# Narrow expert tiles read in whole rows through three 16 KB buffers, gate sums first, then up

## The chip, the cores and the metric

The kernel runs on one core of a Trainium2 chip. The metric is the device time of one execution in microseconds. Weights are read from HBM by the core's 16 DMA engines into SBUF (128 partitions), TensorE (PE) multiplies into eight PSUM banks, ScalarE (ACT) and VectorE (DVE) work on the results, GpSimd (POOL) does little here, and SyncE (SP) issues the weight transfers, in order, on one queue.

## The reference

Three blocks of transformer layers over 256 rows of width 1024. The change touches the mixture of experts of the second block alone: each row goes to two of eight experts, and each expert is a gated product with an inner width of 3584, in fp32.

```python
def swiglu(h, w_gate, w_up, w_down):
    return (jax.nn.silu(h @ w_gate) * (h @ w_up)) @ w_down

def moe_swiglu(h, w_router, we_gate, we_up, we_down):
    t = h.reshape(b * s, d)
    logits = (t @ w_router).astype(F32)
    top_val, top_idx = lax.top_k(logits, TOP_K)
    gates = jax.nn.softmax(top_val, axis=-1)
    combine = jnp.einsum('tk,tke->te', gates, jax.nn.one_hot(top_idx, N_EXPERTS, dtype=F32))
    for e in range(N_EXPERTS):
        y = y + combine[:, e:e + 1].astype(t.dtype) * swiglu(t, we_gate[e], we_up[e], we_down[e])
```

An expert's weights are 1024 x 3584 for gate and for up, 3584 x 1024 for down: 3 x 14 MB, 42 MB in all (1 MB is 1,048,576 bytes in this text).

## The kernel before

**Tiles.** The kernel sorts the rows by expert and works on tiles, each of one expert. A *wide* tile holds up to 128 rows and multiplies in three products of split operands: ACT makes a high part `WH` of each weight chunk (L1397), DVE the low part `WL` (L1401), PE takes WH with XTH, WL with XTH, WH with XTL (L567 to L569). A *narrow* tile holds up to 64 rows and multiplies the fp32 weights as they lie in the ring. The order is wide 0, narrow 0, wide 1, narrow 1, wide 2, narrow 2, narrow 3, narrow 4; each of the eight tiles reads its expert's 42 MB.

**Ring.** `ring` has six slots of 8 KB a partition (1 MB). A tile is read in 42 chunks of 1 MB. The order (`moe_order`) goes by pairs of column blocks: of pair 0 the gate chunks, then the up chunks; of pair 1 gate, up, then the down chunks of pair 0; and so on; pair 3 is half as wide. A gate or up chunk of pairs 0 to 2 is two blocks of 128 rows by 1024 columns, pieces of 4 KB; of pair 3 four blocks by 512 columns, pieces of 2 KB; a down chunk is two adjacent rows of 1024 a partition, 8 KB in one piece. SP issues a chunk when its slot is free: in a wide tile when DVE has made the low part of what lay there (`lo_made`), in a narrow one when PE has used it (`n_eaten`).

**Narrow tile.** For each pair p PE makes the gate sums into one bank (L3322), the up sums into another, and in between turns the columns of the pair before (L3333); ACT takes silu of the gate sums (L2175) and copies the turned columns (L2168), DVE multiplies with the up sums (L2686); PE makes the output sums of the pair before into bank 6 (L3345). In the gaps of this order stand the small steps of the other tiles: adding a wide or narrow tile's result to the rows (*scatter*, L1626 and L1622, with DVE's additions at L1634), and picking the rows of the next tiles (*selection*, L3303 for a wide tile, L3295 for a narrow one). Results of narrow tiles wait in four buffers `NY`, hidden columns in `NHID` and `NHT`.

**Wide tile 1** begins with the selection for narrow tile 1 (`first_of_1`), wide tile 2 without one.

Of the kernel before, what the change touches and what calls it, by code (L numbers as in the profile page):

```python
# [118 lines left out]
def build(nc, t):  # L119
    ctx = ExitStack()  # L120
    with ctx:
# [13 lines left out]
        QT = sb("QT", [128, 8, S])  # L135
        KT = sb("KT", [128, 8, S])
# [10 lines left out]
        neg_tri = sb("neg_tri", [128, 128])  # L147
        neg_ones = sb("neg_ones", [128, 128])
# [162 lines left out]

        landed = [sem(f"landed{s}") for s in range(RING)]
# [5 lines left out]

        def slot_ap(n, nk, width):
            return ring[:, n % RING, 0:nk * width].rearrange("p (k n) -> p k n", k=nk)  # L320
# [793 lines left out]
        n_landed = list(piece_in.values()) + [lam_in, rel_in]  # L1114
        assert len(n_landed) == RING
        n_landed_0 = [16] * len(piece_in) + [32, 64]
# [23 lines left out]
        IDX = pview(NEXP)  # L1140
        assert at_[0] <= 5120
# [19 lines left out]
        NSEL = P[:, 1, 2048:2176].rearrange("p (t s) -> p t s", t=2)  # L1161
        WSEL = P[:, 1, 2176:2432].rearrange("p (t s) -> p t s", t=2)
        XN32 = [P[:, 1, 1024 + 512 * b:1536 + 512 * b].rearrange("p (k r) -> p k r", k=KD) for b in range(2)]
        QT_FLAT, KT_FLAT = (x[:, :, :].rearrange("p k s -> p (k s)") for x in (QT, KT))
        NHID, NHT = ([QT_FLAT[:, at0 + 512 * b:at0 + 512 * b + 512] for b in range(2)] for at0 in (0, 1024))
        NY = [KT_FLAT[:, 512 * b:512 * b + 512] for b in range(4)]
        NCOMB = [P[:, 1, 2432 + S * b:2432 + S * b + S] for b in range(4)]
        MX = P[:, 1, 4096:5120]
# [450 lines left out]
        def scatter_narrow(out, j, half, tt):  # L1619

            side = slice(64 * half, 64 * half + 64)
            return nc.tensor.matmul(out[:, :], NCOMB[j % 4][side, tt * 128:tt * 128 + 128], NY[j % 4][side, :],  # L1622
                                    start=True, stop=True, skip_group_check=True)
# [21 lines left out]
        TURN_W, TURN_N = (1, 3), (1, 7)  # L1645
        SCATTERS = {0: ["wide"], 1: [0], 2: ["wide"], 3: [1], 4: [2, 3]}
# [10 lines left out]
        def eaten_by(j, key):  # L1657
            return j * MOE_CHUNKS + moe_at[key] + 1

        def pair_width(p):  # L1660
            return 256 * (pairs_[p][1] - pairs_[p][0])
# [20 lines left out]
        def _(sp):  # L1682
            def load(n):
# [3 lines left out]
                if N0 <= n < N0 + RING:  # L1687
                    sp.wait_ge(n_eaten, NARROW * MOE_CHUNKS - RING + n - N0 + 1)
# [55 lines left out]
            def load_wide(w, after_narrow):  # L1744

                e = expert_of(w)
                for c in range(MOE_CHUNKS):
                    n = N0 + c
                    if c < RING and after_narrow is not None:
                        sp.wait_ge(n_eaten, (after_narrow + 1) * MOE_CHUNKS + c - RING + 1)  # L1750
# [4 lines left out]

            def load_narrow(j, after_wide):

                e = expert_of(TILE_MAX + j)
                for c in range(MOE_CHUNKS):
                    n, before = N0 + c, j * MOE_CHUNKS + c - RING  # L1760
                    if c < RING and after_wide is not None:
                        sp.wait_ge(lo_made, after_wide * MOE_CHUNKS + (MOE_CHUNKS + n - RING + 1))
                    elif before >= 0:
                        sp.wait_ge(n_eaten, before + 1)
                    sp.dma_start(slot_ap(n, *expert_chunk(n)), expert_rows(e, c)).then_inc(n_landed[c % RING], 16)
# [184 lines left out]
        def _(act):  # L1950
# [209 lines left out]
            def narrow_tile(j, next_columns, next_splits):  # L2160

                def hidden_copy(p):
                    at_ = len(pairs_) * j + p
                    act.wait_ge(n_T, n_T_0 + at_ + 1)
                    if at_ >= 2:
                        act.wait_ge(n_eaten, eaten_by(*((j, ("down", pairs_[p - 2][1] - 1, 1)) if p >= 2 else
# [1430 lines left out]
```

## Time and profile before

| | us |
|---|---|
| median of 3 runs (lowest, highest) | 1922.06 (1919.86, 1922.43) |
| span of the profiled execution, first to last instruction | 1919.0 |
| PE busy in it | 1791.2 |
| DVE busy, ACT busy | 1019.2, 832.1 |
| granted clock of PE over the span | 0.993 |

The profiled execution's span is 3.06 us under the median of the runs. The eight expert tiles take the stretch from about 680 to 1566 us. The profile's times are from one execution. A busy PE in the profile is not PE at its peak, since matmuls overlap; waits are put down to what came last.

### The profile page before, as it was taken

What the parts mean: (1) busy time and instruction counts of PE and PEld (TensorE: products, weight loads), DVE (VectorE), ACT (ScalarE), POOL (GpSimd) and SP (SyncE); (2) the same over time, 40 slices, a digit from 0 to 9 for tenths busy, and PEclk for the clock granted to TensorE, in tenths of its full rate; (3) what the DMA queues carried; (4) which work ended last, traced back from release to release, by engine and by line L of the source; (5) the groups of instructions that cost most, each with busy time, mean ns of one, the idle gap of its engine ahead of it and who ended that gap; (6) DMA issues with size and microseconds to landing.
All of it is one profiled execution on the core that took longest, in us unless ns stands there. A gap on an engine that the chain in (4) does not pass through costs nothing.

```text
span 1919.0 us, 23227 instructions
## 1 busy us (share of the span) xinstructions
PE 1791.2 (93%) x9052; PEld 1268.1 (66%) x9052; DVE 1019.2 (53%) x1494; ACT 832.1 (43%) x1122; POOL 105.3 (5%) x111
## 2 busy tenths in 40 slices
PE   7999999999999999988998989998787879999998
PEld 5887888888888778535883458823232237888877
DVE  7666676554578698313881158810000124477686
ACT  4544577534356477203770047600000025556564
POOL 0000210000000270000000000000000000200002
PEclk9999999999999999999999999999999999999999
DMA  9863636555543299999999999999999986624500
GB/s 367 311 219 129 213 141 221 186 197 188 185 165 121 91 347 413 341 413 409 396 369 386 408 406 356 363 388 410 412 408 411 412 319 220 218 68 156 181 1 34
DMA packets 169570, 526.74 MB, mean 274 GB/s; under 512 B 12385, under 2 KB 23669, under 8 KB 155126
## 3 DMA queue, kind: packets, MB, share of 16 engines
q1 hardware_dynamic: 164224, 511.91, 70.7%
q10 hardware_dynamic: 3990, 9.15, 1.3%
q0 software_dynamic: 1248, 4.21, 0.7%
q8 instruction: 72, 1.18, 0.2%
q14 instruction: 36, 0.29, 0.0%
HBM read 515.26 MB, written 9.98 MB: 274 GB/s over the span
## 4 chain that ended last, share of the span: by engine, by line
PE 71%; DMA 19%; DVE 6%; ACT 2%; issue 1%; POOL 1%; SPq 0%; POOLq 0%; DVEq 0%; ACTq 0%
PE bank L567 17%; PE bank L569 17%; PE bank L568 17%; DMA ring<-in_od_we_up 7%; DMA ring<-in_od_we_down 6%; PE bank L3322 5%; DMA ring<-in_od_we_gate 5%; PE bank L3345 2%; PE bank L793 2%; PE bank L780 1%; DVE WL L1401 1%; PE bank L385 1%; DVE P L1384 1%; PE bank L813 1%; PE bank L811 1%
## 5 line engine op out<-in xcount | busy, mean ns | idle before, releaser
L1401 DVE TENSOR_TENSOR WL<-ring,WH 128x2048 fp32r<-128x2048 f32 (+1 forms) x260 | 584.5, 2264 | 230.4 <-ACT WH L1397 228.7
L1397 ACT ACTIVATE WH<-ring 128x2048 fp32r<-128x2048 f32 x261 | 491.6, 1895 | 243.5 <-PE bank L569 233.0
L567 PE MATMUL bank<-WH,XTH 128*128 128x512 f32 (+1 forms) x1288 | 509.2, 395 | 20.8 <-DVE WL L1401 15.1
L569 PE MATMUL bank<-WH,XTL 128*128 128x512 f32 (+1 forms) x1288 | 500.9, 389 | 0.0
L568 PE MATMUL bank<-WL,XTH 128*128 128x512 f32 (+1 forms) x1288 | 500.4, 388 | 0.0
L3322 PE MATMUL bank<-ring,P 128*64 128x512 f32 (+1 forms) x1280 | 265.5, 547 | 52.2 <-DMA ring<-in_od_we_up 28.0
L567 PEld LDWEIGHTS bank<-WH,XTH 128*128 128x128 f32 x1288 | 243.4, 189 | 79.3 <-DVE WL L1401 21.6
L569 PEld LDWEIGHTS bank<-WH,XTL 128*128 128x128 f32 x1288 | 243.3, 189 | 50.8
L568 PEld LDWEIGHTS bank<-WL,XTH 128*128 128x128 f32 x1288 | 243.8, 189 | 47.5 <-issue 0.5
L3322 PEld LDWEIGHTS bank<-ring,P 128*64 128x64 f32 x1280 | 84.5, 136 | 220.3 <-issue 100.2
L2686 DVE TENSOR_TENSOR QT<-bank,QT 128x512 f32<-128x512 f32 (+1 forms) x20 | 12.5, 625 | 353.1 <-PE bank L3322 353.1
L2175 ACT ACTIVATE QT<-bank 128x512 f32<-128x512 f32 (+1 forms) x20 | 10.9, 544 | 371.2 <-PE bank L3322 371.2
L3345 PE MATMUL bank<-ring,QT 128*64 128x512 f32 x560 | 132.4, 601 | 19.9 <-DMA ring<-in_od_we_down 19.5
L567 PE MATMUL bank<-WH,HTH 128*128 128x512 f32 (+1 forms) x288 | 109.7, 381 | 0.0
L569 PE MATMUL bank<-WH,HTL 128*128 128x512 f32 (+1 forms) x288 | 108.8, 378 | 0.0
L568 PE MATMUL bank<-WL,HTH 128*128 128x512 f32 (+1 forms) x288 | 108.7, 377 | 0.0
L3345 PEld LDWEIGHTS bank<-ring,QT 128*64 128x64 f32 x560 | 37.1, 136 | 105.7 <-issue 72.0
L840 ACT ACTIVATE scr<-scr,nmax 128x128 f32<-128x128 f32 x120 | 53.2, 444 | 39.4 <-DVE nmax L859 39.4
L661 ACT ACTIVATE P<-bank,stat 128x512 f32<-128x512 f32 x54 | 34.2, 684 | 68.1 <-PE bank L569 67.8
L567 PEld LDWEIGHTS bank<-WH,HTH 128*128 128x128 f32 x288 | 54.2, 188 | 10.8 <-DVE WL L1401 0.5
L569 PEld LDWEIGHTS bank<-WH,HTL 128*128 128x128 f32 x288 | 54.2, 188 | 10.2
L568 PEld LDWEIGHTS bank<-WL,HTH 128*128 128x128 f32 x288 | 54.2, 188 | 9.7
(504 smaller groups left out, 1585.0 us busy)
## 6 DMA issues: line engine op xcount, KB each, us to landing
ring<-in_od_we_gate SPq DMA_DIRECT2D x112, 1024.0 KB, 10.9
ring<-in_od_we_up SPq DMA_DIRECT2D x112, 1024.0 KB, 11.2
ring<-in_od_we_down SPq DMA_DIRECT2D x112, 1024.0 KB, 12.9
ring<-in_w_in SPq DMA_DIRECT2D x18, 1024.0 KB, 9.2
ring<-in_fox_w_in SPq DMA_DIRECT2D x16, 1024.0 KB, 6.4
ring<-in_nsa_w_in SPq DMA_DIRECT2D x14, 1024.0 KB, 4.9
ring<-in_w_ada SPq DMA_DIRECT2D x12, 1024.0 KB, 10.3
ring<-in_ev_w_in SPq DMA_DIRECT2D x12, 1024.0 KB, 5.1
```

What stands on the lines that cost most here:

```text
L385: last = nc.tensor.transpose(self.at(i)[:, j * S + tt * 128:j * S + tt * 128 + 128], src(tt), ident[:, :])
L567: nc.tensor.matmul(out, x[0], wt[0][:, k, :], start=start, stop=False, skip_group_check=check)
L568: nc.tensor.matmul(out, x[0], wt[1][:, k, :], start=False, stop=False, skip_group_check=check)
L569: return nc.tensor.matmul(out, x[1], wt[0][:, k, :], start=False, stop=stop, skip_group_check=check)
L661: last = nc.scalar.activation(dest(tt), self.out(c, tt)[:, 0:width], func, scale=stat[:, self.scale + tt:self.scale + tt + 1] if self.scal ...
L780: last = nc.tensor.matmul(self.score_bank(i)[:, a:a + n], q[:, a:a + 128], k[:, 128 - 128 * t0:256], start=not self.pe_mask, stop=True, sk ...
L793: last = nc.tensor.transpose(bank[6 + j % 2][:, c * 128:c * 128 + 128], self.E[j % 4][:, c * 128:c * 128 + 128], ident[:, :])
L840: last = nc.scalar.activation(e, e, ACT.Exp, bias=nmax[:, i % 4, t0:t0 + 1], scale=-1.0, accum_out=rs[:, g % 2, t0, uu:uu + 1])
L1397: nc.scalar.activation(wh, slot_ap(n, nk, width), ACT.Copy).then_inc(hi_made, 1)
L1401: nc.vector.tensor_tensor(wl, slot_ap(n, nk, width), wh.bitcast(F32), ALU.subtract).then_inc(lo_made, 1)
L3322: last = nc.tensor.matmul(out[64 * side:64 * side + 64, 0:width], XN32[j % 2][:, nk * i + k, :], wt[:, k, width * side:width * side + widt ...
L3345: last = nc.tensor.matmul(bank[6][64 * side:64 * side + 64, :], NHT[at_ % 2][:, at_h:at_h + 64], wt[:, k, 512 * side:512 * side + 512], st ...
```

## The change

Wide tiles stay as they are. In a narrow tile the six slots of the ring become three buffers of two slots, 16 KB a partition (`HOMES`; a fourth and a fifth name are set up but unused, since `home_of` is `c % 3`). Gate and up are read in chunks of 128 whole rows, 14 KB a partition, eight for gate and eight for up; down in chunks of four adjacent rows a partition, 16 KB, six of them, and two of two rows, 8 KB. That makes 24 chunks instead of 42. A buffer is filled when its last user has been eaten; the first narrow chunks after a wide tile wait until both slots of the buffer are free, the first wide chunks after a narrow tile until the last user of the buffer that holds their slot is eaten.

The sums of all four pairs are now made chunk by chunk: gate sums of all columns into banks 0 to 3, then up sums into banks 4 to 6 and the other half of bank 3; only then the four products, the turned columns and the output sums into bank 7. ACT takes the four silus after the last gate chunk. The scatters, the turning of the gates, and the selections stand between the up chunks. The selection for narrow tile 1 moves from the start of wide tile 1 into narrow tile 0. Some buffers move to other places in SBUF, `NY` has two instead of four, so tile 2 scatters two results and tile 4 one.

```diff
+        narrow_order = [(what, k) for what in ("gate", "up") for k in range(KD)]
+        narrow_order += [("down", p, side) for p in range(len(pairs_)) for side in range(2)]
+        home_of = [[c % 3 for c in range(NARROW_CHUNKS)] for i in range(NARROW)]
...
-        SCATTERS = {0: ["wide"], 1: [0], 2: ["wide"], 3: [1], 4: [2, 3]}
+        SCATTERS = {0: ["wide"], 1: [0], 2: ["wide", 1], 3: [2], 4: [3]}
...
+        HOMES = [two_slots(N0 + 2 * d) for d in range(3)] + [QK[:, :, :].rearrange("p k s -> p (k s)"), P[:, 1, 1024:5120]]
...
                     if c < RING and after_narrow is not None:
-                        sp.wait_ge(n_eaten, (after_narrow + 1) * MOE_CHUNKS + c - RING + 1)
+                        sp.wait_ge(n_eaten, eaten(*uses(c // 2, after_narrow)[-1]))
...
+            def narrow_rows(e, key):
+                if key[0] != "down":
+                    return (gate if key[0] == "gate" else up)[e, 128 * key[1]:128 * key[1] + 128, :].rearrange("e p n -> p (e n)")
+                n = 2 * pair_width(key[1])
+                k0 = 1024 * key[1] + n // 2 * key[2]
+                return down[e, k0:k0 + n // 2, :].rearrange("e (p k) n -> p (e k n)", p=128)
...
-                for c in range(MOE_CHUNKS):
-                    n, before = N0 + c, j * MOE_CHUNKS + c - RING
-                    if c < RING and after_wide is not None:
-                        sp.wait_ge(lo_made, after_wide * MOE_CHUNKS + (MOE_CHUNKS + n - RING + 1))
-                    elif before >= 0:
-                        sp.wait_ge(n_eaten, before + 1)
-                    sp.dma_start(slot_ap(n, *expert_chunk(n)), expert_rows(e, c)).then_inc(n_landed[c % RING], 16)
+                for c, key in enumerate(narrow_order):
+                    d = home_of[j][c]
+                    before = uses(d, j, c)
+                    if d < 3 and after_wide is not None and d not in home_of[j][:c]:
+                        sp.wait_ge(lo_made, after_wide * MOE_CHUNKS + (N0 + MOE_CHUNKS - RING + 2 * d + 2))
+                    elif before:
+                        sp.wait_ge(n_eaten, eaten(*before[-1]))
+                    ap = narrow_rows(e, key)
+                    sp.dma_start(HOMES[d][:, 0:ap.shape[1]], ap).then_inc(n_landed[d], 16)
...
+                act.wait_ge(n_eaten, eaten_by(j, ("gate", KD - 1)))
+                for p in (LAST, 0, 1, 2):
+                    nc.scalar.activation(NHID[p], hidden_bank("gate", p)[:, 0:pair_width(p)], ACT.Silu).then_inc(n_silu, 1)
+                next_columns()
                 for p in range(len(pairs_)):
...
+                    act.wait_ge(n_T, n_T_0 + len(pairs_) * j + p + 1)
+                    nc.scalar.activation(NHID[p], turned_bank(p)[:, 0:pair_width(p)], ACT.Copy).then_inc(n_hT, 1)
...
+                dve.wait_ge(n_eaten, eaten_by(j, ("up", KD - 1)))
+                dve.wait_ge(n_silu, n_silu_0 + len(pairs_) * (j + 1))
                 for p in range(len(pairs_)):
...
+                    nc.vector.tensor_tensor(NHID[p], hidden_bank("up", p)[:, 0:pair_width(p)], NHID[p], ALU.mult).then_inc(n_mul, 1)
...
+                for k in range(KD):
+                    hidden_sums("gate", k)
...
+                for k in range(KD):
+                    hidden_sums("up", k)
+                    if k == 0:
+                        pe.wait_ge(n_silu, n_silu_0 + len(pairs_) * (j + 1))
+                    if k < len(steps):
+                        scatter(k)
+                    if k == len(steps):
+                        pe.wait_ge(n_selg, n_selg_0 + j + 1)
                         for tt in range(TT):
...
+                    at_ = k - len(steps) - 1
+                    if at_ in (0, 2) and at_ // 2 < len(picks):
+                        if at_ == 0:
+                            pe.wait_ge(ns_added, steps_made(j + 1))
+                        picks[at_ // 2]()
+                turn_hidden_columns(0)
+                for p in range(len(pairs_)):
+                    if p < LAST:
+                        turn_hidden_columns(p + 1)
+                    for of in range(2):
+                        output_sums(p, of)
...
-            narrow_tile(0, 2, [lambda: select_wide(1)])
-            wide_tile(1, first_of_1, nothing)
+            narrow_tile(0, 2, [lambda: select_wide(1), lambda: narrow_after_wide(1, 1)])
+            wide_tile(1, lambda: after_narrow(0, 2), nothing)
```

How this moves PE's instructions is seen in narrow tile 0. First its middle, before: sums of one pair (`ring,P`: weights and the tile's rows), turned columns (`ident,QT`), output sums (`ring,QT`), with the scatters (L1626) and the selection for wide tile 1 (L3303) among them.

```order
L3322 MATMUL bank<-ring,P 64x512 x16
L1626 MATMUL bank<-P 128x512 x2
L3345 MATMUL bank<-ring,QT 64x512 x16
L1626 MATMUL bank<-P 128x512 x2
L3322 MATMUL bank<-ring,P 64x512 x16
L3333 MATMUL bank<-ident,QT 128x128 x4
L3322 MATMUL bank<-ring,P 64x512 x16
L3303 MATMUL bank<-P,O 128x128 x16
L3345 MATMUL bank<-ring,QT 64x512 x16
```

The same stretch after, from up chunk 1 on (L3349 are the sums of a chunk, six instructions of 512 and two of 256 columns; L1648 is the scatter, L3404 turns the gates, L3330 and L3322 are the selections for wide tile 1 and narrow tile 1).

```order
L1648 MATMUL bank<-P 128x512 x2
L3349 MATMUL bank<-ring,P 64x512 x6
L3349 MATMUL bank<-ring,P 64x256 x2
L3404 MATMUL bank<-ident,P 128x128 x2
L3349 MATMUL bank<-ring,P 64x512 x6
L3349 MATMUL bank<-ring,P 64x256 x2
L3330 MATMUL bank<-negs,O 128x128 x16
L3349 MATMUL bank<-ring,P 64x512 x6
L3349 MATMUL bank<-ring,P 64x256 x2
L3349 MATMUL bank<-ring,P 64x512 x6
L3349 MATMUL bank<-ring,P 64x256 x2
L3322 MATMUL bank<-scr,O 128x64 x16
```

Between two small steps there now stands one chunk of the up sums, and both selections lie in this tile.

Second, PE at the end of narrow tile 0 and the start of wide tile 1 (L567), before:

```order
L3322 MATMUL bank<-ring,P 64x256 x16
L3333 MATMUL bank<-ident,QT 128x128 x4
L3322 MATMUL bank<-ring,P 64x256 x16
L3345 MATMUL bank<-ring,QT 64x512 x8
L3333 MATMUL bank<-ident,QT 128x128 x2
L3345 MATMUL bank<-ring,QT 64x512 x16
L3295 MATMUL bank<-P,O 128x64 x16
L567 MATMUL bank<-WH,XTH 128x512
```

And after (L3361 turns the hidden columns, L3369 are the output sums, L584 begins wide tile 1):

```order
L3349 MATMUL bank<-ring,P 64x512 x6
L3349 MATMUL bank<-ring,P 64x256 x2
L3361 MATMUL bank<-ident,P 128x128 x8
L3369 MATMUL bank<-ring,P 64x512 x16
L3361 MATMUL bank<-ident,P 128x128 x4
L3369 MATMUL bank<-ring,P 64x512 x16
L3361 MATMUL bank<-ident,P 128x128 x2
L3369 MATMUL bank<-ring,P 64x512 x24
L584 MATMUL bank<-WH,XTH 128x512
```

All output sums now follow the last up chunk, and between them and wide tile 1 there is no selection any more.

## Rows read from the trace of the kernel before

**Rows 1.** The page: span, and the chain's shares by engine.

```profile
span 1919.0 us, 23227 instructions
...
PE 71%; DMA 19%; DVE 6%; ACT 2%; issue 1%; POOL 1%; SPq 0%; POOLq 0%; DVEq 0%; ACTq 0%
```

**Rows 2.** Windows: stretch, its length, each engine's busy us, PE's clock, DMA share, GB/s.

```profile
890.00:1014.50 124.50, 123.23 (x570) 101.39 (x570) 105.61 (x61) 87.70 (x57) 0.00 (x0) 1.00 1.00 386
...
1246.00:1353.00 107.00, 93.38 (x444) 33.19 (x446) 9.10 (x20) 5.73 (x10) 0.00 (x0) 1.00 1.00 398
1353.00:1460.00 107.00, 88.55 (x424) 30.30 (x422) 6.94 (x13) 5.04 (x9) 0.00 (x0) 1.00 1.02 411
```

**Rows 3.** Waits of PE and SP, 1246 to 1566: us in total, times, longest.

```profile
PE bank L3322 <- DMA ring<-in_od_we_up: 17.9, 32, 1.2
PE bank L3322 <- DMA ring<-in_od_we_gate: 17.8, 29, 1.5
...
SPq L1765 <- PE bank L3322: 172.7, 84, 5.3
```

**Rows 4.** PE's timeline: start, length, instruction, idle time before and its releaser.

```profile
1074.59 1.94 PE L3322 MATMUL bank<-ring,P 128*64 128x512 f32 x8 [0.62 <-DMA ring<-in_od_we_up]
1077.14 1.94 PE L3322 MATMUL bank<-ring,P 128*64 128x512 f32 x8 [0.62 <-DMA ring<-in_od_we_up]
...
1431.94 1.95 PE L3322 MATMUL bank<-ring,P 128*64 128x256 f32 x16 [0.67 <-DMA ring<-in_od_we_gate]
...
1437.35 1.95 PE L3322 MATMUL bank<-ring,P 128*64 128x256 f32 x16 [0.67 <-DMA ring<-in_od_we_up]
...
1442.32 1.94 PE L3345 MATMUL bank<-ring,QT 128*64 128x512 f32 x8 [0.46 <-DMA ring<-in_od_we_down]
...
1452.26 1.94 PE L3345 MATMUL bank<-ring,QT 128*64 128x512 f32 x8 [0.46 <-DMA ring<-in_od_we_down]
```

**Rows 5.** DMA packets of 1353 to 1460, counted by size.

```profile
DMA packets 10618, 43.95 MB, mean 411 GB/s; under 512 B 669, under 2 KB 669, under 8 KB 8821
```

**Rows 6.** DMA issues of 1247.5 to 1249 (queue empty): count, size, us to landing.

```profile
ring<-in_od_we_up SPq DMA_DIRECT2D x1, 1024.0 KB, 5.0
```

**Rows 7.** SP's timeline: the issue into the sixth slot before narrow tile 0.

```profile
786.16 0.37 SPq L1765 DMA_DIRECT2D ring<-in_od_we_up  x1
```

**Rows 8.** PE's timeline: first and last chunks of narrow tiles.

```profile
789.88 7.09 PE L3322 MATMUL bank<-ring,P 128*64 128x512 f32 x32
...
888.45 1.94 PE L3345 MATMUL bank<-ring,QT 128*64 128x512 f32 x8 [0.46 <-DMA ring<-in_od_we_down]
...
1014.44 7.09 PE L3322 MATMUL bank<-ring,P 128*64 128x512 f32 x32
...
1245.93 7.09 PE L3322 MATMUL bank<-ring,P 128*64 128x512 f32 x32
...
1344.60 1.94 PE L3345 MATMUL bank<-ring,QT 128*64 128x512 f32 x8 [0.47 <-DMA ring<-in_od_we_down]
...
1560.17 1.94 PE L3345 MATMUL bank<-ring,QT 128*64 128x512 f32 x8 [0.46 <-DMA ring<-in_od_we_down]
```

**Rows 9.** PE's timeline: a scatter of narrow tile 0, a selection of narrow tile 1.

```profile
824.03 1.98 PE L1626 MATMUL bank<-P 128*128 128x512 f32 x4
...
1079.01 3.84 PE L3303 MATMUL bank<-P,O 128*128 128x128 f32 x32
```

**Rows 10.** Lines of 1353 to 1460: count, busy us, mean ns, idle before.

```profile
L2686 DVE TENSOR_TENSOR QT<-bank,QT 128x512 f32<-128x512 f32 x3 | 2.1, 692 | 71.9 <-PE bank L3322 71.9
...
L2168 ACT ACTIVATE QT<-bank 128x512 f32<-128x512 f32 x3 | 1.8, 598 | 0.4 <-PE bank L3333 0.3
```

**Rows 11.** PE's timeline: last chunk of narrow tile 1, first matmul of wide tile 2.

```profile
1113.13 1.94 PE L3345 MATMUL bank<-ring,QT 128*64 128x512 f32 x8 [0.45 <-DMA ring<-in_od_we_down]
1120.43 0.80 PE L567 MATMUL bank<-WH,XTH 128*128 128x512 f32 x1 [5.36 <-DVE WL L1401]
```

**Rows 12.** Windows: the start of wide tile 2, columns as in rows 2.

```profile
1118.00:1124.80 6.80, 4.37 (x10) 3.47 (x11) 6.47 (x3) 3.87 (x3) 0.00 (x0) 0.50 1.03 410
```

## What the change will do to the time: the prediction

> **What bounds the kernel now.** I first read the page's span and chain [rows 1]: TensorE holds 71% of the chain that ends last, DMA 19%. Then busy time by stage, to see where that DMA part lies [rows 2]: in the wide tile from 890 to 1014.5 TensorE is busy 123.23 of 124.50 us, so TensorE sets its pace; in the narrow tiles it is busy 93.38 and 88.55 of 107, while the DMA share is 1.00 and 1.02. The waits of the last three narrow tiles [rows 3] agree: TensorE waits for weights (17.9 us for up, 17.8 for gate), and SyncE waits 172.7 us for TensorE to free a buffer: all buffers are handed out, the transfers are the limit. So a narrow tile gains what its 42 MB arrive earlier, and a wide tile gains only if its first weights arrive earlier. Before, first matmul to arrival of the last chunk takes 98.6 us in the narrow tiles that follow a wide one (888.45 − 789.88, 1113.13 − 1014.44, 1344.60 − 1245.93); narrow to narrow, last arrival to last arrival takes 107.7 and 107.9 (1344.60, 1452.26, 1560.17) [rows 4, 8, 11]. I call the tiles N0 to N4, the wide ones between them W1 and W2.
>
> **Longer rows.** How fast rows of each length arrive is seen where TensorE waits for each chunk, so that its starts are the arrivals [rows 4]. One MB takes 2.55 us in 4 KB pieces (1074.59 to 1077.14), 2.705 in 2 KB pieces (1431.94 to 1437.35, two chunks) and 2.485 in 8 KB rows (1442.32 to 1452.26, four). A chunk is spread over 16 engines: 16, 32 and 8 pieces each. From 8 to 32 pieces the time grows by 0.22 us: 9.2 ns a piece, and the middle value lies on that line. Without pieces a MB would take 2.485 − 8 × 0.0092 = 2.411. That descriptors of 8 KB really go as one packet is seen in the packets of a tile [rows 5]: 10618 less 8821 leaves 1797 of 8 KB or more, the 14 down chunks × 128.
> The change reads gate and up in 14 KB rows, 16 chunks of 1.75 MB with 8 pieces an engine: 1.75 × 2.411 + 0.074 = 4.293 us each. Six down chunks of 2 MB in 16 KB rows: 4.896. Two of 1 MB as before: 2.485. Together 68.7 + 29.4 + 5.0 = 103.0 us a tile, against 24 × 2.55 + 4 × 2.705 + 14 × 2.485 = 106.8. That is 3.8 a tile, 19 for five, if nothing is lost. No row shows a packet of 14 KB; from below, the 8 KB rate would bound a tile at 42 × 2.485 = 104.4, from above 4 KB's at 107.1. I take the line through three lengths.
> The Trainium skill (DMA: Bandwidth & Descriptors, Where 436 GB/s comes from) puts a ceiling of 435 GB/s on the 16 ports. At that rate a tile's 44.0 MB would take 101.2 us by estimate, 1.8 less than my line; the rows above stay below it.
>
> **Three buffers instead of six: the gaps.** A refill is late unless it is issued early enough: a chunk issued on an empty queue lands 5.0 us later [rows 6], of which 2.55 is its transfer, so 2.45 are start-up. TensorE takes 7.09/4 = 1.77 us a MB plus 0.17 to drain (1.94 for one MB alone) [rows 4, 8], so 3.27 for a gate chunk and 3.7 for a 2 MB down chunk. In the steady state two chunks are queued behind the one that is used (8.6 us), so it may lag by 8.6 − 3.27 − 2.45 = 2.8 us before the DMA runs dry. Five places:
> 1. *Entry from a wide tile.* A buffer needs two slots free; the last was freed at 786.16, 3.7 us ahead of N0 [rows 7], so three buffers land by 792.9 but the fourth chunk can be issued only when the first is used: 3.3 + 2.45 + 4.29 = 10.05 after the tile's start. The 20 that follow take 85.8, so the last lands 95.9 after the start, against 98.6: a gain of 2.7, not 3.8.
> 2. *Up sums.* The scatters and selections now all stand among the up chunks. In N0 and N1: two scatters of 2.0 us, a transpose of 0.45 and two selections of 3.8 [rows 9], 12 us against the 1.2 that each chunk gives back. The lag reaches 3.4 after the first selection and 4.7 after the second; over the allowed 2.8 (4.0 beside the longer down chunk) that is 0.6 + 0.7 = 1.3 us of DMA gap. N2 has four scatters and one selection: 1.5. N3 has two and one: 0.5. N4: none. That takes it that ACT and DVE keep up with the steps.
> 3. *From up to down.* DVE's product (0.69), four transposes, ACT's copy (0.6) [rows 10] and semaphores stop TensorE for some 2.5 us where before they lay beside other sums. The next chunk lands 1.6 us after the up sums anyway, three chunks are under way: nothing for the DMA.
> 4. *Exit.* Behind the last 2 MB chunk only two of 1 MB are queued, 4.97 us; it is used 3.75 after it lands, plus 0.15 for SyncE and 2.45: 1.4 us gap after each of the five tiles.
> 5. *Clock.* W1 began with a selection that filled the wait for its first split weights; this goes to N0. W2 has no such step now: TensorE idles 5.36 us there, the granted clock falls to 0.50 (1.2 GHz) [rows 11, 12], and ten matmuls take 4.37 us, not ten times 0.22 (32 alike in 7.09 [rows 8]): some 2.1 lost in a tile that TensorE bounds. W1 will idle about 6 us, so I expect the same there: +2.1.
>
> **The sum.** N0: −2.7 + 1.3 + 1.4 = 0. W1: +2.1. N1: 0, less 0.4 because ACT no longer is late for W2's first chunk: −0.4. N2: −2.7 + 1.5 = −1.2. N3: 1.4 + 103.0 + 0.5 against 107.7: −2.8. N4: 1.4 + 103.0 against 107.9: −3.5. After N4 the first weights of the next layer come 1.3 later, and two small chunks behind a large one leave TensorE 0.4 later: +1.7. Sum −4.1 us. The span of 1919.0 becomes 1914.9; the median of the runs lies 3.06 above the span, so 1922.06 becomes **1918.0**.
>
> **The rivals.**
> A, the forecast: long packets pay 19, gaps and the clock eat most. For it: three lengths on a line; against: gaps are small differences of long times. Start-up of 2.3 to 2.6 and a W1 without clock drop move it from −8 to −2: 1914 to 1920.
> B, *the DMA never runs dry*: the gaps 2 and 4 (4.6 + 7) and the clock (2.1) vanish as well: −4.1 − 13.7 = −18: 1904. It needs a start-up under 1 us behind a queue, and the rows have 2.45 only on an empty one.
> C, *the gain ends at 8 KB*: 104.4 a tile, +1.4 × 5: +2.9 on balance: 1925. For it: no row holds longer packets.
> D, *slower: the up phase starves the ring*. TensorE's queue is in order: if a scatter or selection waits for DVE's additions or ACT's copies, the up chunks behind it stay unread, the buffers stay full and the DMA stops. Every us beyond the lag of 2.8 is lost one for one. With 2.5 us at each of the six selections' waits: +15, 1933. It decides from 8 us in all, since 4.1 is gained before. For it: before, these steps stood between whole phases, now one chunk (3.1 us) lies between them. Against: DVE is busy only 9 of 107 us [rows 2].
> E, *it doesn't do what it says*: rows are cut into 4 KB packets again; the tile takes 107.1, +4.1 × 5: 1939. Against: 8 KB goes whole [rows 5].
>
> **How the numbers follow.** About 0.2% (3.8 us) is what can be told from no change here. A 0.50, of it 0.33 below 1918.2 and 0.17 within; B 0.12, faster; C 0.15, within 0.12 and slower 0.03; D 0.16, slower 0.13 and within 0.03; E 0.07, slower. Faster 0.45, same 0.32, slower 0.23. The range leaves out half of B, half of D and E, and takes in C: 1906 to 1928.
>
> **What would show it.** Packets of 14336 and 16384 B in the narrow tiles, and up chunks every 4.3 us; 4.35 speaks for C, 4.46 for E. N3 and N4 near 105 and 104.4 from last to last arrival. TensorE's first gate chunks of N0 without a wait for three chunks only. A DMA gap of about 1.4 at each tile's end, and one behind the selections; if TensorE waits there for DVE or ACT, it is D. A clock of 0.50 at W1's start. I am wrong if the chunks don't arrive faster than 8 KB ones, or if the gaps are under 0.5 or over 3 us a tile.

## The result and the profile after

The changed kernel takes **1939.72 us** (median of five runs, 1935.5 to 1948.09) against 1922.06 (1919.86 to 1932.04, five runs beside it): ratio **1.010, 95% interval 1.0068 to 1.0133**. It is slower, and the forecast of 1918.0 (1906 to 1928) missed: direction and range. In the page of the changed kernel, span and chain, which answer to [rows 1], TensorE's share grew and DMA's shrank, although the tiles are longer:

```profile
span 1944.6 us, 22907 instructions
...
PE 73%; DMA 16%; DVE 6%; ACT 3%; issue 1%; SPq 0%; POOLq 0%; POOL 0%; DVEq 0%; ACTq 0%
```

The profiled execution took 1946.36 us itself, one of the longer of the five, and its span is 25.6 us above the one of before, where the medians differ by 17.7. Between the stages' first and last matmuls the 25.6 lie so:

| stage | before | after | difference |
|---|---|---|---|
| N0 | 100.5 | 104.6 | +4.1 |
| W1 | 118.7 | 120.8 | +2.1 |
| N1 | 100.6 | 104.6 | +4.0 |
| N2 to N4 | 316.2 | 327.0 | +10.8 |
| W0, which the change doesn't touch | 123.7 | 125.5 | +1.8 |
| from a tile's last sum to W1, to W2 and to the next layer | 21.4 | 24.1 | +2.7 |

W2 is the same (125.1 and 125.0: its clock fell before too, [rows 12]). W0 lies between 123.7 and 125.6 in the profiled runs of the kernels below, whatever they change. The rest is in the narrow tiles and their borders. The windows over N0, N1 and N3 of the changed kernel (stretch, length, each engine's busy us, PE's clock, DMA share, GB/s) answer to [rows 2]:

```profile
792.60:897.30 104.70, 91.32 (x457) 37.21 (x456) 10.71 (x26) 7.00 (x18) 0.00 (x0) 0.98 0.95 388
...
1023.70:1128.40 104.70, 90.00 (x457) 36.58 (x456) 10.71 (x26) 6.99 (x17) 0.00 (x0) 0.98 0.95 384
...
1365.00:1477.50 112.50, 90.59 (x426) 34.58 (x424) 6.75 (x13) 4.71 (x9) 0.00 (x0) 0.94 0.97 392
```

Before, the DMA share in the narrow tiles was 1.00 to 1.02, the clock 1.00, the rate 397 to 411 GB/s. Now the DMA runs dry: 0.95 to 0.97, and 384 to 392 GB/s. TensorE isn't the bound either, busy 90 of 104.7 us. TensorE's and SyncE's waits over N2 to N4 (us in total, times, longest) answer to [rows 3]:

```profile
PE bank L3349 <- DMA ring<-in_od_we_gate: 30.8, 15, 4.3
PE bank L3349 <- DMA ring<-in_od_we_up: 15.0, 11, 3.6
PE bank L3369 <- DMA ring<-in_od_we_down: 12.1, 13, 2.7
...
SPq L1810 <- PE bank L3349: 209.6, 48, 8.9
```

Both wait: TensorE for weights (30.8 us in the gate sums, before 17.8), and SyncE for TensorE to hand back a buffer (209.6, before 172.7). Both waited before too, but with the DMA always busy; now they wait while it runs dry. That points to a ring that is too short. How a gap looks is seen in TensorE's timeline, here N3's first gate chunks and its last up chunk (start, length, instruction, idle time before and its releaser):

```profile
1370.82 7.93 PE L3349 MATMUL bank<-ring,scr 128*64 128x512 f32 x32 [4.30 <-DMA ring<-in_od_we_gate]
1379.29 3.23 PE L3349 MATMUL bank<-ring,scr 128*64 128x512 f32 x16 [0.54 <-DMA ring<-in_od_we_gate]
1385.78 12.10 PE L3349 MATMUL bank<-ring,scr 128*64 128x512 f32 x48 [3.27 <-DMA ring<-in_od_we_gate]
1399.74 3.23 PE L3349 MATMUL bank<-ring,scr 128*64 128x512 f32 x16 [1.86 <-DMA ring<-in_od_we_gate]
...
1441.98 4.92 PE L3349 MATMUL bank<-ring,scr 128*64 128x512 f32 x16 [3.58 <-DMA ring<-in_od_we_up]
```

The chunk at 1385.78 comes 6.49 us after the one before it, not 4.29. TensorE had idled 4.30 us ahead of 1370.82; with the clock at 0.50 right after it, two chunks took 7.93 us, where two take 6.2 at full clock. The first buffer came back late, and three chunks on, where its next chunk is awaited, TensorE idles 3.27 us, and three further on 1.86.

I call a *gap* what a chunk lands later than the chunk before it plus its own transfer (4.29, 4.89 or 2.47 us). In the changed kernel's five narrow tiles the gaps over 0.3 us, from the fourth chunk of N0 to N2 on and over all of N3 and N4, add up to some 38 us: 5.5 at the fourth chunk of N0 to N2, 10.5 in the gate sums behind it, 11.5 in the up sums, 5.6 in the down sums, 4.9 at the tiles' last and first chunks. The kernel with four buffers, below, has 3.2.

### The profile page after: what moved, and what is told of

The parts are those of the page before. It is cut to its first block, busy times and chain, and to the rows that moved or that the text cites. A ratio compares the mean times of both kernels' runs of the same rounds, so it can differ in the third digit from the quotient of the medians.

```text
span 1944.6 us, 22907 instructions
## 1 busy us (share of the span) xinstructions
PE 1794.0 (92%) x9052; PEld 1284.8 (66%) x9052; DVE 1019.9 (52%) x1494; ACT 830.2 (43%) x1122; POOL 101.7 (5%) x111
## 4 chain that ended last, share of the span: by engine, by line
PE 73%; DMA 16%; DVE 6%; ACT 3%; issue 1%; SPq 0%; POOLq 0%; POOL 0%; DVEq 0%; ACTq 0%
PE bank L584 17%; PE bank L586 17%; PE bank L585 17%; PE bank L3349 8%; DMA ring<-in_od_we_down 5%; DMA ring<-in_od_we_up 5%; DMA ring<-in_od_we_gate 5%; PE bank L3369 2%; DVE WL L1423 2%; PE bank L810 1%; PE bank L797 1%; ACT WH L1419 1%; PE bank L3322 1%; PE bank L402 1%; DVE P L1406 1%
## 5 line engine op out<-in xcount | busy, mean ns | idle before, releaser
L584 PE MATMUL bank<-WH,XTH 128*128 128x512 f32 (+1 forms) x1288 | 510.5, 396 | 28.0 <-DVE WL L1423 22.6
L584 PEld LDWEIGHTS bank<-WH,XTH 128*128 128x128 f32 x1288 | 244.5, 190 | 87.9 <-DVE WL L1423 23.9
L3349 PE MATMUL bank<-ring,P 128*64 128x512 f32 (+1 forms) x768 | 158.4, 561 | 35.5 <-DMA ring<-in_od_we_gate 27.1
L1656 DVE TENSOR_TENSOR X<-bank,X 128x512 f32<-128x512 f32 x28 | 18.0, 685 | 287.2 <-PE bank L1644 203.5
L3369 PE MATMUL bank<-ring,P 128*64 128x512 f32 x560 | 130.5, 610 | 22.0 <-DMA ring<-in_od_we_down 21.6
L3349 PEld LDWEIGHTS bank<-ring,P 128*64 128x64 f32 x768 | 54.2, 141 | 140.6 <-issue 99.1
L3349 PE MATMUL bank<-ring,scr 128*64 128x512 f32 (+1 forms) x512 | 107.5, 570 | 27.0 <-DMA ring<-in_od_we_gate 17.1
L2213 ACT ACTIVATE P<-bank 128x512 f32<-128x512 f32 (+1 forms) x20 | 10.9, 544 | 233.7 <-PE bank L3361 233.6
L584 PE MATMUL bank<-WH,HTH 128*128 128x512 f32 (+1 forms) x288 | 109.7, 381 | 0.0
L3369 PEld LDWEIGHTS bank<-ring,P 128*64 128x64 f32 x560 | 43.9, 139 | 98.1 <-issue 93.2
L3349 PEld LDWEIGHTS bank<-ring,scr 128*64 128x64 f32 x512 | 37.1, 143 | 97.5 <-issue 67.5
L2209 ACT ACTIVATE P<-bank 128x512 f32<-128x512 f32 (+1 forms) x20 | 9.3, 550 | 177.4 <-PE bank L3349 177.4
```

The costliest lines, as they stand in the source:

```text
L584: nc.tensor.matmul(out, x[0], wt[0][:, k, :], start=start, stop=False, skip_group_check=check)
L3349: last = nc.tensor.matmul(hidden_bank(what, p)[64 * side:64 * side + 64, 0:width], XN32[j % 2][:, k, :], wt[:, 1024 * p + width * side:102 ...
L3369: last = nc.tensor.matmul(bank[7][64 * side:64 * side + 64, :], NHID[p][:, r * 128 + 64 * of:r * 128 + 64 * of + 64], wt[:, D * r + 512 * ...
```

## The experiments

Theory after the result: **three buffers hold too little ahead; every late use of a chunk empties the DMA queue.** Rivals: the new order of the sums does it; the clock that falls in the gaps does it; the long rows themselves do it. A fourth, code that is read beside the weights, was not tried by itself.

**Five buffers.** The two further homes stand in the code already and are unused.

```diff
-        home_of = [[c % 3 for c in range(NARROW_CHUNKS)] for i in range(NARROW)]
+        home_of = [[c % 5 for c in range(NARROW_CHUNKS)] for i in range(NARROW)]
```

> The changed kernel with one line more: the narrow tiles' chunks go round five 16 KB buffers (the fourth and fifth name that the change sets up) instead of three. Theory 1, three buffers are too few, so that each late refill is felt: with four chunks behind the one in use a refill may come 8.6 us later, the gaps at the exits, behind the selections and at the entry from a wide tile vanish, the narrow tiles come to about 103 to 105 us from last to last arrival, TensorE never idles 4 us in them and its clock stays at 1.0: about 1912 us, 25 to 30 under the changed kernel. Rival, the gaps come from TensorE's order (all gate sums, then up sums with the small steps among them) or from code loads whatever the depth: at most 10 us under the changed kernel, about 1930.

Measured 1905.36 us (1903.31 to 1909.24), ratio 0.9923 (0.9907 to 0.994): faster than both kernels, 34 us below three buffers, 7 below what I expected. N0, N1, N3 and N4 in its windows:

```profile
788.80:886.00 97.20, 89.11 (x457) 36.76 (x456) 10.72 (x26) 7.00 (x17) 0.00 (x0) 1.00 1.01 426
1011.70:1109.30 97.60, 88.00 (x457) 36.02 (x456) 10.72 (x26) 7.00 (x17) 0.00 (x0) 1.00 1.01 425
1337.30:1441.70 104.40, 86.55 (x428) 33.51 (x424) 6.75 (x13) 4.72 (x9) 0.00 (x0) 0.98 1.00 422
1441.70:1545.80 104.10, 83.48 (x396) 29.41 (x392) 5.55 (x10) 4.71 (x9) 0.00 (x0) 0.98 1.00 422
```

The same rows, sums, scatters and selections in the same order, and the DMA share is 1.00 again, at 422 to 426 GB/s. So the order of the sums is not what holds the DMA up. The clock didn't stay at 1.00, as I had expected: it is 0.98 in N3 and N4.

**Six buffers of 8 KB, the changed order.** The three 16 KB buffers are cut into six; gate and up rows come as 8 KB and 6 KB, and each piece is awaited and handed back by itself.

```diff
-        narrow_order = [(what, k) for what in ("gate", "up") for k in range(KD)]
+        narrow_order = [(what, k, h) for what in ("gate", "up") for k in range(KD) for h in range(2)]
...
-        home_of = [[c % 3 for c in range(NARROW_CHUNKS)] for i in range(NARROW)]
+        home_of = [[c % 6 for c in range(NARROW_CHUNKS)] for i in range(NARROW)]
...
-        HOMES = [two_slots(N0 + 2 * d) for d in range(3)] + [QK[:, :, :].rearrange("p k s -> p (k s)"), P[:, 1, 1024:5120]]
+        HOMES = [ring[:, slot_at(N0 + d), :] for d in range(6)]
```

> The changed kernel's order of sums, but the ring is six slots of 8 KB as before: a gate or up chunk is cut into 2048 and 1536 columns (pieces of 8 and 6 KB), a down chunk into two rows a partition (8 KB). 46 chunks a tile. Theory 1, the size of the refill against the ring: five small chunks lie behind the one in use, a refill may be late by some 6 us instead of 2.8, so the gaps vanish but for the entry; a tile takes about 104.7 at these lengths: near 1920, 15 to 20 under the changed kernel. Rival, the order of sums makes the gaps: within 5 us of the changed kernel's time.

Measured 1918.43 us (1916.32 to 1919.64), ratio 0.999: 21 us below the changed kernel with the same 48 KB of buffers and the same order. The rival of the order falls a second time.

**Idle matmuls in TensorE's waits.** They keep the clock up where TensorE waits: 9 before N3 and N4, 11 before W1 and W2.

```diff
+            def busy(count):
+                for _ in range(count):
+                    nc.tensor.matmul(bank[2][:, :], ident[:, :], O[:, 0, 0:512], start=True, stop=True, skip_group_check=True)
...
+                if j >= 3:
+                    busy(9)
                 for k in range(KD):
                     hidden_sums("gate", k)
...
                 pe.wait_ge(ns_added, steps_made(j + 1))
+                busy(11)
```

> The changed kernel with idle matmuls on TensorE (128x512 into a bank that nobody reads): nine before the first gate chunk of narrow tiles 3 and 4 (about 4.0 us, the time that TensorE waits there), eleven before the first matmul of wide tiles 1 and 2 (4.8 us of a wait of 5.3 to 6.3). They compute nothing that is used. Theory 2, the clock: TensorE falls to half after these waits, eats the next chunks slower, and that makes the next gap; with fillers it stays at 1.0 there: wide tiles 1 and 2 gain 2.1 each, the second and third gaps of narrow 3 and 4 (2.2, 1.1, 1.8, 1.1 us) shrink by 4 to 5 in all: about 9 under the changed kernel, near 1931. Rival, the clock is no cause of the gaps, only the depth of the ring is: 4 under it at most (wide tiles alone), and the gaps in narrow 3 and 4 as they were.

Measured 1945.67 us (1942.09 to 1946.28), ratio 1.0126 (1.011 to 1.0143), not the 1931 that the clock as main cause would give. The kernel was mis-sized, as TensorE's timeline before W1 shows:

```profile
896.87 9.71 PE L3337 MATMUL bank<-O,ident 128*128 128x512 f32 x22
906.01 0.79 PE L584 MATMUL bank<-WH,XTH 128*128 128x512 f32 x1
```

The eleven run as 22 and take 9.1 us, where the wait was 5.3: counted from the tile before, W1 starts 3.8 us later and W2 2.7, which eats the 1.7 us that each of the two tiles is shorter (119.0 and 123.3 against 120.8 and 125.0). In N3 and N4 they fit, and N2 to N4 take 5.1 less, 321.9. So I shortened them:

**Shorter idle matmuls.** 5 before N3, N4, W1 and W2, and 4 ahead of the fourth chunk of N0 to N2 (these fall on one of the four gate sums, which loses its first three chunks there).

```diff
                 for k in range(KD):
+                    if j >= 3 and k == 0:
+                        busy(5)
+                    if j < 3 and k == 3:
+                        busy(4)
                     hidden_sums("gate", k)
...
                 pe.wait_ge(ns_added, steps_made(j + 1))
+                busy(5)
```

> The changed kernel with three buffers, and idle matmuls in TensorE's waits, sized shorter than the waits: 5 (4.2 us) before the first chunk of N3 and N4 and before W1 and W2, 4 (3.3 us) before the fourth chunk of N0 to N2. The idle matmuls' sums are overwritten. Theory that the clock's fall makes the later gaps: the falls to 0.50 in N0 to N4 and at W1 and W2 vanish, W1 and W2 take 1.7 us less each, N2 to N4 5 to 7 us less, N0 and N1 1: about 1929 to 1931. Rival, the clock only falls where the DMA has already run dry, and the gaps come from three buffers: 1936 to 1940.

Measured 1934.75 us (1932.72 to 1940.39), ratio 1.0087 (1.0062 to 1.0113): between the two expectations, and its interval overlaps that of the changed kernel. The trace says more. TensorE at N3's start:

```profile
1360.34 4.56 PE L3337 MATMUL bank<-O,ident 128*128 128x512 f32 x10
1365.46 3.23 PE L3353 MATMUL bank<-ring,scr 128*64 128x512 f32 x16 [0.57 <-DMA ring<-in_od_we_gate]
1369.76 3.23 PE L3353 MATMUL bank<-ring,scr 128*64 128x512 f32 x16 [1.06 <-DMA ring<-in_od_we_gate]
1374.06 3.23 PE L3353 MATMUL bank<-ring,scr 128*64 128x512 f32 x16 [1.07 <-DMA ring<-in_od_we_gate]
```

Chunks come every 4.3 us, and the waits of 3.27 and 1.86 that the changed kernel had at the fourth and seventh are gone: the chain of clock, late hand-back and next gap is broken here. N2 to N4 take 319.8 us, 7.2 less. With four buffers they take 305.6. So the clock's fall multiplies the gaps and doesn't make them. Its price in the narrow tiles, 5 to 7 of the 34 us, rests on one profiled execution of each kernel; the medians differ by 5.0, W1 and W2 included.

**Selection back at W1's start**, where it stood before, out of N0's up sums.

```diff
...
-            narrow_tile(0, 2, [lambda: select_wide(1), lambda: narrow_after_wide(1, 1)])
-            wide_tile(1, lambda: after_narrow(0, 2), nothing)
+            narrow_tile(0, 2, [lambda: select_wide(1)])
+            wide_tile(1, first_of_1, nothing)
```

> The changed kernel with the selection for narrow tile 1 back at the start of wide tile 1, as before the change. Theory of the prediction's steps 2 and 5: the selection fills TensorE's wait, the clock stays at 1.0 at the start of wide tile 1 (2.1 us), and narrow tile 0 loses the gap behind its second selection (1.4): 3 to 4 under the changed kernel, about 1936. Rival, the place of the selection does not matter: within 1 us of it.

Measured 1940.91 us (1934.61 to 1943.18), ratio 1.0096: no difference. W1 starts 6.1 us after N0's end instead of 5.3, and its clock falls to 0.50 at 899.9 all the same.

**Four buffers.** As with five, with `c % 4`.

> Four 16 KB buffers in place of three, all else as in the changed kernel. Theory: the loss is lag. With three buffers a chunk may be used 2.8 us late before the DMA runs dry; a fourth adds one chunk, 4.29 us, so 7.1. The largest gaps in the changed kernel's five narrow tiles are 2 to 4.5 us, so nearly all go, and the time is within 2 us of five buffers: 1905 to 1908. Rival, each buffer brings a like share (from 1939.7 with three to 1905.4 with five): about 1922. Rival, the order of the sums holds the DMA up: above 1930.

Measured 1905.28 us (1903.85 to 1910.5), ratio 0.9925 (0.9908 to 0.9943): the same as five. Three buffers lose 34 us and the fourth gives it all back, so it is a threshold, not a share for each buffer. The fourth buffer isn't a slot of the ring, so its chunk doesn't wait for the wide tile either; TensorE at N0's start uses it, in `QK`, without a wait:

```profile
791.66 9.24 PE L3349 MATMUL bank<-ring,P 128*64 128x512 f32 x48
800.73 3.18 PE L3349 MATMUL bank<-QK,P 128*64 128x512 f32 x16
803.93 3.23 PE L3349 MATMUL bank<-ring,P 128*64 128x512 f32 x16
808.23 3.23 PE L3349 MATMUL bank<-ring,P 128*64 128x512 f32 x16 [1.06 <-DMA ring<-in_od_we_gate]
```

**A late use, added.** 5 idle matmuls into a free bank ahead of the second up chunk of each narrow tile, with three buffers and with four.

```diff
                 for k in range(KD):
+                    if k == 1:
+                        late(5)
                     hidden_sums("up", k)
```

> The changed kernel with three buffers, and in each narrow tile 5 idle matmuls (4.2 us, into a bank that is free there) ahead of the second up chunk: each later chunk of the tile is used that much later. Theory that the loss is lag: three buffers have none to spare, TensorE gives back 1.2 us a chunk only while the DMA is behind it, so the most of 4.2 us is lost in each of five tiles: 1939.7 + 12 to 21 = 1952 to 1961. Rival, the lag of 2.8 us that the prediction allowed is there in the up sums and takes the first 2.8 of the 4.2: 1939.7 + 5 by 1.4 = 1947 or less. Rival, the loss is elsewhere: 1940.

> The same 5 idle matmuls (4.2 us) in each narrow tile, with four buffers. The fourth adds 4.29 us to the lag that is allowed: theory, little of it is lost, 1905.3 + 0 to 5 = 1905 to 1910. Rival, TensorE's own time decides by now: 1905.3 + 21 = 1926.

With three buffers 1955.76 us (1953.65 to 1962.06), ratio 1.0194 (1.0174 to 1.0213): 16 us more, 3.2 of the 4.2 added in each tile. The allowance of 2.8 us is not there. N4 shows it best, where the up sums had no gap over 0.3 us: with the late use they have two, of 3.0 and 1.2, the whole of the 4.2. With four buffers they have none. With four 1916.24 us (1911.52 to 1926.77): 11 more than without, where I expected 0 to 5. So the fourth buffer covers what the kernel needs and, by these runs, about half of 4.2 us beyond; the threshold is close.

**Five buffers, shorter rows.** The same bytes into the same buffers by two DMAs a chunk, 8 KB and 6 KB, or 8 and 8.

```diff
...
-                    ap = narrow_rows(e, key)
-                    sp.dma_start(HOMES[d][:, 0:ap.shape[1]], ap).then_inc(n_landed[d], 16)
+                    at_ = 0
+                    for ap in parts_of(e, key):
+                        sp.dma_start(HOMES[d][:, at_:at_ + ap.shape[1]], ap).then_inc(n_landed[d], 16)
+                        at_ += ap.shape[1]
```

> Five 16 KB buffers, each chunk read by two DMAs: gate and up rows of 14 KB as 8 KB and 6 KB, the four adjacent down rows of 16 KB as 8 KB twice. Buffers, order and bytes as with five buffers and whole rows (1905.4). Theory of the prediction, 9.2 ns for each piece: 16 chunks by 8 pieces an engine and 6 chunks by 8 more, 176 by 9.2 ns = 1.6 us a tile, 8 us for five tiles: 1913. Rival, rows over 8 KB bring nothing: 1905 to 1907. Packets of 14336 and 16384 bytes are then gone.

Measured 1913.16 us (1911.35 to 1914.81), ratio 0.9966 (0.9953 to 0.9979): 7.8 us above five buffers with whole rows, forecast 8.0 (6.0 above their second measurement, below). Rows over 8 KB are worth about what the line through three lengths says, while the DMA never waits.

**Three buffers, shorter rows.** The same edit on the changed kernel: the buffers are still awaited and handed back whole.

> Three 16 KB buffers, each filled by two DMAs of 8 KB and 6 KB (or 8 and 8) a row, handed back only when the whole buffer is read. Against six 8 KB buffers (1918.4) the memory, the DMAs and the order of the sums are the same, and only the unit in which a buffer is awaited and handed back is doubled; against the changed kernel (1939.7) only the rows are shorter. Theory that the unit of three large buffers costs the loss, whatever the rows: 1939.7 + 8 (the pieces, as with five buffers) = 1945 to 1950. Rival, long rows themselves make a transfer land late behind a queue (longer start-up, engines that finish apart): near six buffers, 1918 to 1930.

Measured 1940.37 us (1936.61 to 1941.37), ratio 1.0089. Neither expectation. Against six small buffers, which have the same bytes, DMAs and order, it is 22 us slower: that is the price of the unit in which a buffer is awaited and handed back. N0 in the windows of both, first these three buffers, then the six small ones:

```profile
790.60:895.60 105.00, 90.15 (x457) 37.03 (x456) 10.72 (x26) 6.99 (x18) 0.00 (x0) 1.00 0.95 383
...
791.80:891.70 99.90, 90.91 (x457) 35.50 (x456) 10.72 (x26) 7.00 (x17) 0.00 (x0) 1.00 0.98 403
```

Against the changed kernel it is the same, though its pieces cost 8 more; so with three buffers the long rows lose elsewhere what they gain. From the fourth chunk on N3 and N4 have 1.3 and 0.5 us of gaps in place of 7.3 and 2.8; why, these runs don't tell.

**Idle matmuls before W1 and W2, five buffers.** `busy(5)` where the eleven stood.

> Five buffers, and 5 idle matmuls (4.2 us) in TensorE's waits of some 5 us before W1 and W2. The idle matmuls' sums are overwritten. If the fall of the clock there costs what the prediction says (2.1 us in each): 1905.4 less 4 = 1901. Rival, the cost is hidden behind the weights' splitting on ACT and DVE: 1905.

> Five buffers with 5 idle matmuls ahead of W1 and W2 once more, beside five buffers without them on the same chip. If the clock's fall at these two starts costs some 2 us each: 4 us below five buffers alone. Rival, something that differs from run to run is larger (its runs lay at 1900.6, 1904.5 and 1909.5 to 1912.0): no difference between the two that the runs can tell.

> Five 16 KB buffers alone, beside the last one: 1905 again, and 15 us below before.

The first time 1909.52 us (1900.57 to 1911.96), ratio 0.9942; the second 1903.10 (1901.89 to 1911.41), 0.9923 (0.9907 to 0.9939), beside five buffers alone at 1907.17 (1904.36 to 1916.37), 0.9945 (0.9928 to 0.9963). In the profiles W1 takes 118.8 against 120.7 us and W2 123.1 against 125.8, so 4.6 us are there; but the runs of the same kernel spread over 11 us, and the intervals overlap. Not settled. The version that surely beats both kernels is the change with four or five buffers, 0.55 to 0.77% below before in three measurements.

## Why the prediction was wrong

- **What bounds the kernel: right.** The narrow tiles wait for their weights; with five buffers, where those come sooner, N0 takes 97.2 us instead of 100.5 while W1 gains nothing (120.4 instead of 118.7).
- **Longer rows: right, to a few per cent.** A narrow tile of the changed kernel in packets, which answers to [rows 5]:

```profile
DMA packets 3463, 44.14 MB, mean 392 GB/s; under 512 B 384, under 2 KB 384, under 8 KB 384
```

  3463 packets in place of 10618, none of them of 2 to 8 KB: rows go whole. Gate and up chunks come every 4.29 to 4.30 us where nothing disturbs them (1365.46, 1369.76, 1374.06 above; 4.293 forecast), 16 KB ones every 4.89 (4.896). In the kernel with five buffers N3 and N4 take 104.4 and 104.1 us from last to last arrival, with one gap in each (1.6 and 1.1); 103.0 was forecast without gaps. Five buffers with shorter rows price the pieces at 7.8 for 8.0. Rivals C and E are out. The Trainium skill (DMA: Bandwidth & Descriptors, Where 436 GB/s comes from) sets 435 GB/s as ceiling of the ports; the 422 to 426 of five buffers stay below it, as the forecast had it.
- **Three buffers instead of six: the step that failed.** Its arithmetic allowed a chunk to be used 2.8 us late: 8.6 in the queue, less 3.27 of use, less 2.45 of start-up. The start-up was read from a 1 MB chunk in 4 KB pieces on an empty queue [rows 6]. Two issues of the changed kernel, the first on an empty queue (796.03), the second (1432.42) 2.67 us before the chunk ahead of it had landed (count, size, us to landing):

```profile
ring<-in_od_we_gate SPq DMA_DIRECT2D x1, 1792.0 KB, 7.2
...
ring<-in_od_we_up SPq DMA_DIRECT2D x1, 1792.0 KB, 9.5
```

  Empty: 7.16 − 4.29 = 2.87, 0.4 more than I took; eight chunks issued on a queue that was empty, or within 1.3 us of it, took 2.8 to 3.4. Behind a queue: 9.51 − 4.29 = 5.22, of it 2.67 until the chunk ahead had landed.
  I call *lead* the time from a chunk's issue to the landing of the chunk ahead of it. The undisturbed lead is as forecast, 5.2 to 5.3 us (8.6 − 3.27). What a start needs of it was too small. In the five narrow tiles, behind the fourth chunk, 100 chunks have a lead of more than 2 us, and sixteen of them land over 0.6 us late:
  - Of the 16 with a lead of 2 to 4 us, ten are late. One has code beside it (a packet on the instruction queue, see *Gate sums*). The other nine took 3.4 to 5.2 us from issue, less their own transfer, 4.3 on average. With 4.3 in place of 2.45 the allowance is 1.0 us by estimate, not 2.8; the added 4.2 us with three buffers, of which 3.2 a tile were lost, say the same.
  - Of the 84 with a lead of 4 us or more, six are late. All six have code beside them, as 15 of the 84 have. The forecast had no term for that.

  The Trainium skill (SBUF — State Buffer, The DMA setup-cost knee) has a fixed cost of about 2 us, the same for any size; here it was 2.45 for 4 KB rows, 2.8 to 3.4 for 14 KB ones, and no constant behind a queue.
  How a chunk comes late is seen in its packets. A chunk is spread over 16 engines, and each writes a 4-byte packet when its share is done; the chunk has landed with the last one. Of the chunk issued at 1432.42 fifteen lie between 1438.24 and 1439.51, the sixteenth at 1441.61; the other engines go on with the next chunk meanwhile. That this spread makes the loss is not shown: three buffers with shorter rows have less of it (last section) and are no faster.
  - *Entry.* Fourth chunk 10.05 us after the tile's start: 10.6 in N0 and N1 (803.24 − 792.62), 12.5 in N2.
  - *Up sums.* Gaps of 1.3, 1.3, 1.5, 0.5 and 0: measured 11.5 in the up sums and 5.6 in the down sums behind them, 17 for 4.6. TensorE steps through scatter and selections without a wait for ACT or DVE, as forecast; the size was off.
  - *Gate sums.* Forecast none, measured 10.5 us. They follow on the gaps at the tile's start and the clock (next). Code comes beside eight gaps of the five tiles, up and down sums among them: a packet of 16 KB on the instruction queue, on one engine, between the landing of the chunk ahead, less 1 us, and the late one. Six of the eight are 1.4 to 1.7 us each, 9.4 in all, with the packet 2.1 to 2.5 us ahead of the landing: N0's eighth, N1's tenth and twentieth, N2's seventh, fourteenth and twentieth chunk. Code is read as often in before and with four buffers (72 packets in each span). With four, two gaps stand beside it, of 0.95 and 1.5; in before, away from the tiles' starts, four of 0.8 to 1.3, at chunks with a lead of 7.6 us or more. That code makes the gap was not tried by itself.
  - *From up to down*: nothing, right (0.79 us for DVE's product). *Exit*: 1.4 forecast; N3's and N4's first chunks have 1.95 and 1.52.
- **The clock: right at W1, missed in the narrow tiles.** W1's start and N3's gate sums, windows as above, which answer to [rows 12]:

```profile
900.10:906.90 6.80, 4.32 (x10) 3.46 (x11) 6.17 (x3) 3.82 (x3) 0.00 (x0) 0.50 1.03 413
...
1384.80:1391.60 6.80, 5.82 (x16) 1.94 (x18) 0.00 (x0) 0.00 (x0) 0.00 (x0) 0.50 0.98 420
```

  W1 took the 2.1 us more that were forecast (118.7 to 120.8). But the clock is 0.50 (1.2 GHz) in eleven places of these stages, one before; nine of them are in narrow tiles, where I had every matmul at full clock. The idle matmuls price that at 5 to 7 us, as far as one execution of each kernel tells.
- **The sum.** Gaps inside the tiles were forecast at 4.6 us, besides entry and exit; they are 27.6. The difference, 23, is most of the 29.7 by which the profiled span (1944.6) lies above the forecast one (1914.9); the medians' miss is 21.7. Rival B, a DMA that never runs dry, is what the change gives with a fourth buffer: 1904 forecast, 1905.3 measured. That these agree so well is in part luck: B had no clock loss at W1, and with four buffers the clock still falls there, to 0.50 at 892.6. Rival D has the right sign and nearly the time (1933), but TensorE waits for weights there, not for ACT or DVE, and over a third of these gaps lie in the gate sums, where D had none.

## What to carry to other kernels

Longer rows in fewer, larger buffers trade rate for depth: price both, and count the depth in chunks that stay queued when the consumer is late, not in bytes. Before taking an allowance from one start-up on an empty queue, look for chunks that were issued behind others: how early each was issued, whether it came late, and what else the DMA engines read just then. A kernel that stops at the edge of its buffers is told by three signs at once: the consumer waits for data, the issuer waits for a buffer, and the DMA share is under 1 all the same. The first two alone stand in the kernel before as well, whose DMA is full. One buffer more is the cheapest test.

## What the runs showed of the hardware

- The engines that share a chunk end apart. From the median of its sixteen 4-byte packets to the last it takes 1.7 us in the changed kernel (117 of the 120 narrow chunks, those whose packets don't mix with a neighbour's), 1.8 with four buffers (115), where it costs nothing, and 1.3 with three buffers and shorter rows (224 of 230), which are no faster.
- A transfer's start on an empty queue is slower for long rows: 2.45 us with 4 KB, 2.8 to 3.4 with 14 KB; and in the chunk issued at 796.03 the first packets take 0.8 to 1.6 us each, where a 14 KB packet takes 0.54 later.
- Beside one 16 KB packet of code a chunk can land 0.8 to 1.7 us late even with a lead of 4 us or more (changed kernel) or 7.6 us or more (before). That the packet is the cause was not tried.
- A DMA that pauses can slow TensorE twice: it waits, and in nine places of the changed kernel's narrow tiles what follows runs at 0.50 of the clock, so that 16 sums of a gate or up chunk take 4.7 to 4.9 us instead of 3.2.
